# A hybrid encoder block on eight cores: the attention stage issued from one list of finer pieces, the key weights' load waiting for the first tile, and a new order of the prefix

## The chip, the cores and the metric

The kernel runs on all 8 cores of one Trainium2 chip, as one launch. Each core has a matrix engine (TensorE, PE in the profile), a vector engine (DVE), a scalar engine (ACT), a general engine (GpSimd, POOL) and a queue engine (SP) that issues transfers; transfers that convert float32 to bfloat16 on the way are issued by POOL. The engines run their own programs in order and wait for each other by semaphores. The time is that of the slowest core, in microseconds of the device; the kernel before had a median of 2082.74 us over 3 runs (2081.79, 2082.74 and 2295.69).

## The reference, cut to what matters

The input x has 4 sequences of 2048 tokens and 2048 channels. The part of the block that the change touches is the first half of the token mixer:

```
h = rms_norm(x, g_pre_mix)
a_x, a_b, a_c, q, k, v, og, a_lr, gate_a, gate_b = split(h @ w_in)
y_a = (a_b * causal_conv3(a_c * a_x)) @ w_a_out
log_a = log_sigmoid(a_lr @ w_alpha_up + b_alpha_up) / 16     # forget gate
b = cumsum(log_a) in chunks of 64 tokens
att = where(lower, (q e^(b-mid)) (k e^(mid-b))^T, (q e^(mid-b)) (k e^(b-mid))^T)
state = e^(b_last) * state + (k e^(b_last-b))^T v             # from chunk to chunk
o = rms_norm(att v + (q e^b) state) * head_gain * silu(og)
y_b = o @ w_b_out
x = x + rms_norm((sigmoid(gate_a) y_a + sigmoid(gate_b) y_b) @ w_mix_out)
```

There are 4 heads with keys of 128 and values of 256 channels. A SwiGLU mixer (5632 wide) and a gated embedding layer follow; the change doesn't touch them.

## The kernel before, in words

**Work of a core.** Two cores share a sequence. Each computes 1024 tokens, its own half. The second half needs the attention state that the first half leaves, so every core also reads the 1024 tokens before its own (`xp`, zeros on the first core of a pair), and forms only their decayed keys and from them the state: this is the **prefix**. The order of everything is that of the Python program: `P.emit` appends an instruction to its engine's program and works out the semaphores from the buffers that it reads and writes (`_needs`, L70). So the program text fixes both the order within each engine and which wait stands in front of which instruction.

**Prefix (L404 to L660).** Sixteen tiles of 128 tokens are loaded by SP, the 8 of `xp` first (numbers 0 to 7, tokens 512 to 1023 before tokens 0 to 511), then the 8 of `x`. A load is issued when the tile four before it was normalised (`t_norm`, L480). A string `ORDER` (L653) is walked word by word: S is a tile's square sum on ACT, X its scaling on DVE, T its 16 transposes on PE (two banks), V the two evictions on DVE, L and A the gate projection, z, c and e the gate, its scan and its factor for one head, a and b the keys of one head for the first and the second two tiles of a half (16 matmuls of 256 columns each), k and f the decayed keys and their transposes, G one of 16 products of prefix tokens with decayed keys (8 matmuls of 512 columns, evicted by ACT), D the four parts of the first decay (`Decay.one` to `four`), W the load of the query weights, C four small constants. The key weights come in four loads on POOL's queue (L501 to L504), followed on the same queue by the first value weights.

**Attention (L670 to L917).** `seed` forms the states of two heads. Then 4 steps (2 head pairs x 2 halves of the tokens) are run. A step has 12 **dense blocks** of 16 matmuls x 512 columns: q and k for two heads, 4 of v, 4 of the output gate og. The og blocks of a step run in the next step. Beside them it has 8 **units** (one head x 128 tokens): `near` (L797) is two score matmuls and two state updates on PE, then on DVE the mask, two copies and two updates of the state; `far` (L828) is three matmuls, then a square sum and rstd on ACT; `gated` is one DVE instruction that frees the bank of `far`; `out_flip` transposes for two heads. Each decay (`Decay`, L545) has one float32 matmul, ACT and DVE work and feeds the next q and k blocks; one set of factor tiles serves all. Dense blocks take turns on banks 0, 1, 2 (`dense`), all else on banks 3 to 7 in turn (`little`): a bank is handed out again five requests later and must be free by then.

Before, the loop at L875 ties these small pieces to numbered slots: a slot is one dense block, pieces registered by `ahead` are emitted in front of it, those by `after` behind it. `near` of a unit is in slot g, `far` in slot g+2, `gated` at the head of slot g+3.

**Convolution (L919 to L967).** For 8 channel groups and 2 halves three dense blocks each (x, C, B). The last step's og blocks and small pieces run into it. Weights come through a ring of 36,864 bytes per partition (`wload`), a load waiting for the readers of what it overwrites.

## Time and profile before

| | |
|---|---|
| median of 3 runs | 2082.74 us |
| the profiled execution's time | 2082.87 us |
| its span on the slowest core (core 6) | 2081.3 us |
| spans of the eight cores | 2064.5 to 2081.3 us |
| PE busy in the span | 1991.4 us (96%) |
| DVE, ACT, POOL busy | 582.5, 477.6, 155.4 us |
| mean granted clock of TensorE, by core | 0.989 to 0.993 |

The span is from the first to the last instruction of a core. PE idle is what is left beside its busy time, some 90 us of 2081. In this execution the prefix takes the first 133 us, attention runs up to about 388 us, and the convolution, whose first blocks stand among its last pieces, to about 520 us.

### The profile page before, as it was taken

To read this page: it belongs to the slowest core of one execution; us is meant where nothing else is said; L and a number is where in the kernel's file an instruction comes from. 1 tells how busy PE (TensorE), PEld (TensorE's weight loads), DVE (VectorE), ACT (ScalarE), POOL (GpSimd) and SP (SyncE) were. 2 spreads that over 40 slices of the span, in tenths; PEclk is the share of its full clock that TensorE was granted. 3 is DMA by queue.
4 is the path that set the end of the run, shared out by engine and by line. 5 is a ranking of instruction groups with operands and counts; after the bars stand their busy time and mean duration, and the time that the engine had idled before them with its cause. 6 is when DMAs were issued, how large, how long until landed. Compare 5 with 4: busy or idle time off the path is not lost.

```text
span 2081.3 us, 25824 instructions; the slowest of 8 cores (2064.5 to 2081.3 us)
## 1 busy us (share of the span) xinstructions
PE 1991.4 (96%) x10064; PEld 942.1 (45%) x10064; DVE 582.5 (28%) x911; ACT 477.6 (23%) x990; POOL 155.4 (7%) x185
## 2 busy tenths in 40 slices
PE   4999999999999999999799999999999999998896
PEld 3644455444444444444344444444444444444342
DVE  4836665433211111216310111110110011006416
ACT  4744553100111111116300000100000011014655
POOL 0011111000000000000000000000000000000233
PEclk9999999999999999999999999999999999999998
DMA  9830314554454543858564444434443454375353
GB/s 245 197 57 1 58 24 62 92 79 74 70 82 72 81 73 49 162 81 219 142 110 74 74 85 90 92 69 80 81 78 62 81 89 73 72 149 125 73 92 162
DMA packets 49796, 194.21 MB, mean 93 GB/s; under 512 B 3307, under 2 KB 4715, under 8 KB 43660
## 3 DMA queue, kind: packets, MB, share of 16 engines
q0 software_dynamic: 38688, 137.44, 40.0%
q1 hardware_dynamic: 10988, 55.13, 8.2%
q8 instruction: 81, 1.33, 0.2%
q14 instruction: 39, 0.32, 0.1%
HBM read 313.20 MB, written 16.78 MB: 159 GB/s over the span
## 4 chain that ended last, share of the span: by engine, by line
PE 89%; DMA 5%; DVE 3%; issue 2%; ACT 1%; DVEq 0%; POOL 0%; SPq 0%; ACTq 0%; POOLq 0%
PE bank L368 88%; ACT arena L356 1%; DMA arena<-w_ffu 1%; DMA arena<-w_k 1%; PE bank L376 1%; DVE arena L362 1%; DVE arena L359 1%; DMA arena<-w_ple 1%; DMA arena<-w_mix 1%; DMA arena<-xp 0%; DVE arena L407 0%; DVE arena L526 0%; DVE arena L818 0%; DVEq L158 0%; DVE arena L1065 0%
## 5 line engine op out<-in xcount | busy, mean ns | idle before, releaser
L368 PE MATMUL bank<-arena 128*128 128x512 bf16 (+3 forms) x9408 | 1957.9, 369 | 50.4 <-DVE arena L359 11.2
L368 PEld LDWEIGHTS bank<-arena 128*128 128x128 bf16 (+1 forms) x9408 | 899.9, 98 | 1084.2 <-issue 84.5
L359 DVE TENSOR_TENSOR arena<-bank,arena 128x512 f32<-128x512 f32 (+4 forms) x432 | 312.7, 738 | 1380.2 <-PE bank L368 1150.7
L356 ACT ACTIVATE arena<-bank 128x512 f32<-128x512 f32 (+8 forms) x408 | 227.0, 563 | 1482.6 <-PE bank L368 1089.0
L356 ACT ACTIVATE arena<-arena 128x1 f32<-128x1 f32 (+4 forms) x393 | 215.3, 563 | 68.3 <-DMA arena<-xp 18.0
L362 DVE SCALAR_TENSOR_TENSOR arena<-arena 128x512 f32<-128x512 f32 (+3 forms) x73 | 88.8, 1221 | 7.2 <-ACT arena L356 2.2
L344 POOL DMA_DIRECT2D arena<-w_ffu x44 | 31.4, 713 | 610.4 <-PE bank L368 428.9
L376 PE MATMUL bank<-arena 128*128 128x128 bf16 x656 | 51.0, 228 | 21.5 <-DVE arena L407 16.9
L376 PEld LDWEIGHTS bank<-arena 128*128 128x128 bf16 x656 | 44.4, 102 | 36.4 <-issue 26.3
L1364 POOL TENSOR_TENSOR arena<-arena 128x512 f32<-128x512 f32 x31 | 46.1, 1489 | 92.9 <-DVE arena L359 46.1
L362 DVE SCALAR_TENSOR_TENSOR arena<-bank,arena 128x256 bf16<-128x256 f32 (+1 forms) x64 | 33.2, 518 | 51.2 <-ACT arena L356 26.0
L359 DVE TENSOR_TENSOR arena<-arena 128x128 bf16<-128x128 bf16 (+2 forms) x81 | 40.9, 513 | 5.1 <-ACT arena L356 0.9
L344 POOL DMA_DIRECT2D arena<-w_gate x16 | 12.4, 772 | 322.7 <-PE bank L368 322.7
L794 POOL TENSOR_TENSOR arena<-arena 128x256 f32<-128x256 f32 x32 | 23.2, 726 | 140.4 <-DVE arena L359 138.1
L344 POOL DMA_DIRECT2D arena<-w_fd x16 | 11.9, 742 | 290.4 <-PE bank L368 271.0
L362 DVE SCALAR_TENSOR_TENSOR arena<-arena,bank 128x256 f32<-128x256 f32 x64 | 30.7, 480 | 9.3 <-DVE arena L818 4.7
L407 DVE TENSOR_SCALAR arena<-arena 128x2048 bf16<-128x2048 f32 x16 | 20.5, 1281 | 18.3 <-ACT arena L356 18.2
L818 DVE CAST arena<-arena 128x256 bf16<-128x256 f32 x64 | 24.2, 378 | 0.2 <-DVE arena L359 0.2
L356 ACT ACT_TABLE_LOAD x13 | 16.7, 1283 | 32.4 <-PE bank L368 30.3
L526 DVE TENSOR_TENSOR_SCAN arena<-arena 128x512 f32<-128x512 f32 x16 | 19.5, 1217 | 1.4 <-ACT arena L356 1.4
L356 ACT ACTIVATION_READ_ACCUMULATOR arena<-bank 128x1 f32 x96 | 18.8, 196 | 0.0
L344 POOL DMA_DIRECT2D arena<-w_conv x8 | 6.2, 780 | 125.9 <-PE bank L368 105.2
(30 smaller groups left out, 80.0 us busy)
## 6 DMA issues: line engine op xcount, KB each, us to landing
arena<-w_ffu POOLq DMA_DIRECT2D x44, 1024.0 KB, 8.5
arena<-w_gate POOLq DMA_DIRECT2D x16, 1536.0 KB, 13.7
arena<-w_fd POOLq DMA_DIRECT2D x16, 1408.0 KB, 11.1
arena<-x SPq DMA_DIRECT2D x16, 1024.0 KB, 9.7
arena<-w_conv POOLq DMA_DIRECT2D x8, 1536.0 KB, 13.7
arena<-xp SPq DMA_DIRECT2D x8, 1024.0 KB, 12.8
arena<-w_mix POOLq DMA_DIRECT2D x4, 2048.0 KB, 17.2
x1s<-arena SPq DMA_DIRECT2D x8, 1024.0 KB, 12.5
```

The costliest lines, as they stand in the source:

```text
L344: P.dma("pool", f"w{j}", lambda e: e.dma_start(out=flat, in_=src, max_dma_last_dim=8192), writes=[buf, wsems[j]])
L356: P.emit("act", lambda e: e.activation(out=out, in_=in_, func=func, **kw), reads=reads, writes=writes, partw=partw)
L359: P.emit("dve", lambda e: e.tensor_tensor(out=out, in0=in0, in1=in1, op=op), reads=reads, writes=writes, partw=partw)
L362: P.emit("dve", lambda e: e.scalar_tensor_tensor(out=out, in0=in0, scalar=scalar, in1=in1, op0=op0, op1=op1), reads=reads, writes=writes, ...
L368: P.emit("pe", lambda e, l=l, r=r, j=j: e.matmul(out_ap, lhsT=l, rhs=r, start=(start and j == 0), stop=(stop and j == n - 1)), reads=reads ...
L376: P.emit("pe", lambda e, j=j, a=a: e.transpose(out=ptv[:, j * 128:(j + 1) * 128], in_=a, identity=ident), reads=list(reads) + [tb0] if j = ...
L407: P.emit("dve", lambda e: e.tensor_scalar(out=xn, in0=x, scalar1=stats[:, i, 2:3], scalar2=None, op0=ALU.mult), reads=[xbuf, stb[i]], writ ...
L526: P.emit("dve", lambda e: e.tensor_tensor_scan(out=out, data0=data0, data1=data1, initial=0.0, op0=ALU.mult, op1=ALU.add), reads=reads, wr ...
L794: P.emit("pool", lambda e, o=o: e.tensor_tensor(out=o, in0=o, in1=hgb, op=ALU.mult), reads=[cb], writes=[SOb[i]])
L818: P.emit("dve", lambda e, n=n: e.tensor_copy(out=sbf_r[n].ap, in_=S[:, h, :]), reads=[Sb[h]], writes=[sbfb[n]])
L1364: P.emit("pool", lambda e: e.tensor_tensor(out=out, in0=sg, in1=gbs_r[s].ap, op=ALU.mult), reads=[sb_, gbs_b[s]], writes=wr, partw=part)
```

## The change

The key weights' four loads wait for tile 0 in place of tile 1. The prefix's list is a new one; its pieces are the same, in another order. The slots of the attention stage go: their place is taken by a second list, `ORDER2`, walked as the first is. `near` is split: its PE part is N, its DVE part M (`state`); the tail of an og block is l (`og_rest`). F, g, t, K are `far`, `gated`, `out_flip`, `k_flip`; d is a part of a decay, four to each; s a seed; w a weight load (w0 value weights and w1 gate weights of the second head pair, w2 the first convolution weights); Z takes the convolution's memory; X, C, B are its first blocks. The number of a q, k word counts 2 to a step, of v, o, l, t 4, of N, M, F, g 8. The last 36 blocks of the convolution keep their order. The amount of work is the same. Cut to its core:

```diff
-        P.dma("pool", f"wf_wk{h}", lambda e, h=h: e.dma_start(out=wk_r.ap[:, h * 2048:(h + 1) * 2048], in_=w_k[h], max_dma_last_dim=8192), after=[xin[1][1]], writes=[wkb[h]])
+        P.dma("pool", f"wf_wk{h}", lambda e, h=h: e.dma_start(out=wk_r.ap[:, h * 2048:(h + 1) * 2048], in_=w_k[h], max_dma_last_dim=8192), after=[xin[0][1]], writes=[wkb[h]])
...
-    ORDER = """S0 X0 S1 S2 X1 T0 S3 V0 T1 X2 V1 T2 S4 X3 a0 a1 V2 X4 S5 T3 a2 V3 T4 V4 S6 L0 b1 X5 T5 V5 S7 X6 H z0
-        X7 c0 z1 a3 c1 T6 e0 z2 z3 V6 b2 T7 V7 c3 c2 S8 b0 S9 X8 b3 k0 e2 e1 L1 T8 V8 S10 z4 f0 a4 X9 T9 S11 C
-        e3 z5 k1 b4 k2 f2 V9 f1 a5 X10 T10 c4 e4 k3 a6 b6 X11 k4 z6 b5 c5 V10 c6 f3 e5 z7 T11 f4 k5 S12 V11 a7
-        b7 f5 c7 v e6 X12 e7 A0 k6 k7 f6 T12 f7 W S13 E V12 D0 G0 G1 S14 G2 X13 X14 G3 G4 G5 G6 T14 V14 T13 D1
-        G7 S15 V13 G8 D2 G9 G10 X15 G11 G12 T15 G13 V15 G14 A1 G15 D3"""
+    ORDER = """S0 X0 S1 X1 S2 S3 T0 V0 T1 S4 X2 T2 S5 V1 X3 a0 T3 V2 a1 V3 X4 L0 S6 X5 T4 a2 V4 z0 X6 c0 z1 S7 b0 b2 T6 T5 S8
+        c1 e0 V6 e1 X7 z3 b1 V5 T7 V7 k0 k1 z2 c2 S9 H a3 X8 L1 a4 T8 e2 c3 V8 S10 a5 X9 f0 z5 z4 k2 b4 b3 X10 e3 f1 T9
+        a6 c5 S11 f2 C V9 T10 c4 X11 z6 b5 k3 a7 V10 e5 c6 f3 e4 e6 z7 k4 b7 k5 T11 V11 S12 b6 c7 f4 f5 k6 e7 X12 A0 v W
+        k7 f6 f7 T12 S13 E G0 X13 G1 S14 G2 G3 G4 X14 V12 G5 D0 G6 D1 T13 S15 G7 G8 T14 X15 V13 V14 D2 D3 G9 G10 G11 G12
+        T15 G13 V15 G14 G15 A1"""
...
-            def late():
-                tt(sg, bk[:, :], sg, ALU.mult, [bb, SOb[i]], [SOb[i]])
-                for hh in range(2):
-                    o = sg[:, hh * 256:(hh + 1) * 256]
-                    P.emit("pool", lambda e, o=o: e.tensor_tensor(out=o, in0=o, in1=hgb, op=ALU.mult), reads=[cb], writes=[SOb[i]])
-
-            ahead(slot["n"] + 1, late)
+            self.gb[i] = (bk, bb)
+
+        def og_rest(self, i):
+            bk, bb = self.gb[i]
+            sg = SO_r[i].ap
+            tt(sg, bk[:, :], sg, ALU.mult, [bb, SOb[i]], [SOb[i]])
+            for hh in range(2):
+                o = sg[:, hh * 256:(hh + 1) * 256]
+                P.emit("pool", lambda e, o=o: e.tensor_tensor(out=o, in0=o, in1=hgb, op=ALU.mult), reads=[cb], writes=[SOb[i]])
...
+            self.nb[(hh, i)] = us
+
+        def state(self, hh, i):
+
+            h = self.pair * 2 + hh
+            a_, t_ = i % 2, self.unit(hh, i) % 3
+            us = self.nb[(hh, i)]
+            bk, bb, _ = us[0]
...
-    for n, stp in enumerate(steps):
-        stp.wv, stp.wo = wv_of[stp.pair], wo_of.get(stp.pair)
-        mid = [lambda i=i, p=steps[n - 1]: p.og_block(i) for i in range(4)] if n > 0 else [lambda: stp.v_block(0), lambda: stp.v_block(1)]
-        blocks = [lambda: stp.q_block(0), lambda: stp.k_block(0)] + mid + [lambda: stp.q_block(1), lambda: stp.k_block(1)]
-        blocks += [lambda i=i: stp.v_block(i) for i in range(0 if n > 0 else 2, 4)]
-        g0 = slot["n"]
-        q1 = g0 + 2 + len(mid)
-        nxt = g0 + len(blocks)
-        d1 = decays[2 * n + 1]
-        for g, f in ((g0 + 1, lambda d=d1: d.one(little)), (g0 + 2, d1.two), (g0 + 3, d1.three), (q1 - 1, d1.four), (g0 + 3, lambda p=stp: p.k_flip(0)), (q1 + 3, lambda p=stp: p.k_flip(1))):
-            after(g, f)
-        if n < 3:
-            d0 = decays[2 * n + 2]
-            for g, f in ((q1 + 1, lambda d=d0: d.one(little)), (q1 + 2, d0.two), (q1 + 3, d0.three), (nxt - 1, d0.four)):
-                after(g, f)
-        for u, (hh, i) in enumerate([(hh, i) for hh in range(2) for i in range(4)]):
-            g = nxt + 2 + u
-            ahead(g + 3, lambda p=stp, a=hh, i=i: p.gated(a, i))
-            if hh == 1:
-                after(g + 4, lambda p=stp, i=i: p.out_flip(i))
-            after(g + 2, lambda p=stp, a=hh, i=i: p.far(a, i))
-            after(g, lambda p=stp, a=hh, i=i: p.near(a, i))
-        for blk in blocks:
-            pre()
-            blk()
-            run_small()
-        if n == 2:
-            seed(1)
-        if n == 1:
+    conv_w = []
+
+    def load(n):
+        if n == 0:
             load_v(1)
-        if n == 2:
+        elif n == 1:
             load_o(1)
-            steps[2].wo = steps[3].wo = wo_of[1]
...
+    def load(n):
+        if n == 0:
             load_v(1)
-        if n == 2:
+        elif n == 1:
             load_o(1)
-            steps[2].wo = steps[3].wo = wo_of[1]
-    conv_w = [wload(w_conv[0])]
-    for i in range(4):
-        pre()
-        steps[3].og_block(i)
-        run_small()
-
-
-    M.drop(wk_r, wal_r, wq_r, GT_r[1], aug_r)
-    ua_r = M.take_at(B0 + 5632, 16384, BF16, "p (k t) -> p k t", k=8)
-    ua = ua_r.ap
-    uab = ua_r.buf("ua")
-    ux_r = [M.take(2048, F32) for _ in range(2)]
-    uxb = [r.buf(f"ux{j}") for j, r in enumerate(ux_r)]
-    u_r = [M.take(514 * 4, F32) for _ in range(2)]
-    ub_ = [r.buf(f"u{j}") for j, r in enumerate(u_r)]
-    y_r = [M.take(2048, F32) for _ in range(2)]
-    yb = [r.buf(f"y{j}") for j, r in enumerate(y_r)]
-    hal_r = M.take(64, F32)
-    halb = hal_r.buf("hal")
-
-    for cc in range(8):
-        if cc > 0:
-            conv_w.append(wload(w_conv[cc]))
+        else:
+            conv_w.append(wload(w_conv[n - 2]))
...
+    def conv_room(n):
+        M.drop(wk_r, wal_r, wq_r, GT_r[1], aug_r)
+        r = M.take_at(B0 + 5632, 16384, BF16, "p (k t) -> p k t", k=8)
+        cv["ua"], cv["uab"] = r, r.buf("ua")
+        for name, size in (("ux", 2048), ("u", 514 * 4), ("y", 2048)):
+            rs = [M.take(size, F32) for _ in range(2)]
+            cv[name], cv[name + "b"] = rs, [r.buf(f"{name}{j}") for j, r in enumerate(rs)]
+        cv["hal"] = M.take(64, F32)
+        cv["halb"] = cv["hal"].buf("hal")
...
+    def conv_x(cc, half):
+        if cc >= len(conv_w):
+            load(cc + 2)
+        wx, _, _, wb, ts, hb = conv_of(cc, half)
+        bk, bb = dense.next()
+        mm(bk[:, :], bb, [(wx[:, k, :], hT[:, k, ts]) for k in range(16)], [wb, hb])
+        act(cv["ux"][half].ap, bk[:, :], AF.Copy, [bb], [cv["uxb"][half]])
...
+    DO2 = {"q": step_of(Step.q_block, 2), "k": step_of(Step.k_block, 2), "v": step_of(Step.v_block, 4), "o": step_of(Step.og_block, 4),
+           "l": step_of(Step.og_rest, 4), "K": step_of(Step.k_flip, 2), "t": step_of(Step.out_flip, 4),
+           "N": step_of(lambda p, u: p.near(u // 4, u % 4), 8), "M": step_of(lambda p, u: p.state(u // 4, u % 4), 8),
+           "F": step_of(lambda p, u: p.far(u // 4, u % 4), 8), "g": step_of(lambda p, u: p.gated(u // 4, u % 4), 8),
+           "d": lambda n: (lambda: decays[n // 4].one(little), decays[n // 4].two, decays[n // 4].three, decays[n // 4].four)[n % 4](),
+           "s": lambda n: seed(n), "w": load, "Z": conv_room, "X": lambda n: conv_x(n // 2, n % 2), "C": lambda n: conv_c(n // 2, n % 2), "B": lambda n: conv_b(n // 2, n % 2)}
+    ORDER2 = """q0 k0 v0 d4 d5 d6 q1 k1 d7 K0 v2 d8 v1 d9 K1 d10 N0 q2 v6 N1 M0 M1 o0 l0 F0 d11 k2 N2 v3 d12 g0 M2 K2 o1 N3 N4
+        o2 d13 M3 F1 M4 l2 F2 o3 N5 l1 M5 d14 F3 g1 g2 l3 q3 d15 k3 d16 v5 N6 F4 v4 M6 g3 d17 F5 g4 d18 N7 K3 g5 M7 v7
+        N8 M8 q4 F6 g6 d19 F7 k4 g7 t1 d20 w0 t0 t2 d21 o4 F8 l4 d22 q5 t3 o5 g8 N9 M9 l5 o6 N10 M10 o7 N11 M11 N12 F9
+        l6 v9 l7 g9 F10 M12 k5 K4 F11 g10 d23 N13 M13 g11 v10 d24 d25 d26 q6 w1 N14 M14 F12 v8 g12 d27 k6 N15 o8 F13 l8
+        t4 g13 v11 F14 s1 M15 g14 d28 N16 M16 K5 v12 N17 M17 N18 F15 M18 o9 F16 o10 t5 t6 l9 d29 g15 g16 F17 v14 l10 N19
+        M19 t7 F18 d30 g17 o11 g18 N20 F19 M20 q7 K6 F20 N21 l11 v15 g19 g20 o12 N22 M21 M22 t8 l12 v13 d31 N23 F21 g21
+        M23 k7 F22 g22 Z o13 N24 F23 o14 M24 N25 g23 M25 F24 K7 w2 o15 N26 l13 M26 X0 t10 g24 N27 l14 l15 C0 M27 t9 F25
+        B0 N28 M28 g25 F26 g26 X1 C1 N29 M29 F27 t11 F28 g27 B1 F29 g28 N30 g29 X2 M30 N31 M31 C2 F30 t12 B2 g30 F31 X3
+        t14 g31 C3 t15 B3 t13"""
+    for word in ORDER2.split():
+        DO2[word[0]](int(word[1:] or 0))
+    for n in range(4, 16):
+        conv_x(n // 2, n % 2)
+        conv_c(n // 2, n % 2)
+        conv_b(n // 2, n % 2)
```

## Rows read from the trace of the kernel before

**Rows 1.** Page, part 4: shares of the chain that ended last.

```profile
PE 89%; DMA 5%; DVE 3%; issue 2%; ACT 1%; DVEq 0%; POOL 0%; SPq 0%; ACTq 0%; POOLq 0%
```

**Rows 2.** Windows: stretch, length, each engine's busy us, TensorE clock, DMA share, GB/s.

```profile
0.00:40.00 40.00, 13.78 (x92) 10.81 (x93) 15.13 (x16) 18.34 (x30) 4.54 (x10) 1.00 0.93 252
40.00:133.00 93.00, 90.31 (x665) 55.15 (x662) 61.77 (x66) 55.11 (x94) 2.56 (x3) 1.00 0.76 165
133.00:400.00 267.00, 257.68 (x1477) 130.90 (x1478) 156.21 (x349) 111.05 (x278) 35.33 (x51) 1.00 0.28 44
```

**Rows 3.** Waits of PE, whole span: releaser, total us, times, longest.

```profile
PE bank L376 <- DVE arena L407: 16.9, 4, 13.3
...
PE bank L368 <- DMA arena<-w_k: 10.4, 3, 6.4
...
PE bank L368 <- DVE arena L362: 9.1, 11, 1.3
...
PE bank L368 <- ACT arena L356: 1.0, 1, 1.0
```

**Rows 4.** Timeline of PE, prefix: start, us, work, idle before and its releaser.

```profile
13.28 1.86 PE L376 MATMUL bank<-arena 128*128 128x128 bf16 x16 [13.28 <-DVE arena L407]
...
25.46 3.57 PE L368 MATMUL bank<-arena 128*128 128x256 bf16 x16 [3.19 <-DMA arena<-w_k]
35.39 3.57 PE L368 MATMUL bank<-arena 128*128 128x256 bf16 x16 [6.36 <-DMA arena<-w_k]
38.76 1.87 PE L376 MATMUL bank<-arena 128*128 128x128 bf16 x16
41.51 1.91 PE L368 MATMUL bank<-arena 128*128 128x256 bf16 x16 [0.89 <-DMA arena<-w_k]
43.26 1.06 PE L376 MATMUL bank<-arena 128*128 128x128 bf16 x16
44.24 5.47 PE L368 MATMUL bank<-arena 128*16 128x512 bf16 x32
```

**Rows 5.** Timeline of POOL: the key weights' loads.

```profile
13.35 0.73 POOL L504 DMA_DIRECT2D arena<-w_k  x1 [12.65 <-DMA arena<-xp]
...
16.91 0.77 POOL L344 DMA_DIRECT2D arena<-w_v  x1
```

**Rows 6.** Tile w_k: its transfers.

```profile
DMA to landing us min/median/max: 11.9/23.4/31.8
```

**Rows 7.** Timeline of ACT: square sums of two tiles.

```profile
9.04 1.91 ACT L356 ACTIVATE arena<-arena 128x2048 bf16<-128x2048 f32 x1 [6.25 <-DMA arena<-xp]
...
12.82 1.91 ACT L356 ACTIVATE arena<-arena 128x2048 bf16<-128x2048 f32 x1 [1.19 <-DMA arena<-xp]
```

**Rows 8.** Timeline of DVE, prefix.

```profile
39.92 2.35 DVE L359 TENSOR_TENSOR arena<-bank,arena 128x1024 bf16<-128x1024 bf16 x2 [10.03 <-PE bank L376]
```

**Rows 9.** Timeline of PE: end of prefix, and attention.

```profile
133.20 18.63 PE L368 MATMUL bank<-arena 128*128 128x256 bf16 x98 [1.03 <-ACT arena L356]
...
191.95 8.38 PE L368 MATMUL bank<-arena 128*128 128x256 bf16 x46 [0.73 <-DVE arena L362]
201.33 9.54 PE L368 MATMUL bank<-arena 128*128 128x256 bf16 x48 [1.00 <-DVE arena L362]
212.20 0.27 PE L368 MATMUL bank<-arena 128*128 128x256 bf16 x1 [1.33 <-DVE arena L362]
...
212.53 3.62 PE L368 MATMUL bank<-arena 128*128 128x512 bf16 x16
```

**Rows 10.** Timeline of DVE in the same stretch.

```profile
191.32 0.48 DVE L362 SCALAR_TENSOR_TENSOR arena<-bank,arena 128x256 bf16<-128x256 f32 x1 [0.85 <-ACT arena L356]
...
196.06 2.54 DVE L362 SCALAR_TENSOR_TENSOR arena<-bank,arena 128x512 bf16<-128x512 f32 x4
...
200.70 0.48 DVE L362 SCALAR_TENSOR_TENSOR arena<-bank,arena 128x256 bf16<-128x256 f32 x1
```

**Rows 11.** Tile w_conv: its transfers.

```profile
DMA to landing us min/median/max: 13.3/13.7/23.3
```

More of the change, by code:

```diff
@@ L732, in __init__ @@
             self.sb = {}
[L733 removed]
+            self.ob, self.nb, self.gb = {}, {}, {}
             self.ts = slice(self.half * 512, (self.half + 1) * 512)
@@ L804, in near @@
             ts = slice(i * 128, (i + 1) * 128)
-            a_, t_ = i % 2, self.unit(hh, i) % 3
             bk, bb = little.next()
@@ new lines, in step_of, with go @@
+    def step_of(f, per):
+        def go(n):
+            stp = steps[n // per]
+            stp.wv, stp.wo = wv_of.get(stp.pair), wo_of.get(stp.pair)
+            f(stp, n % per)
+        return go
+    cv = {}
+    def conv_room(n):
[7 more added lines that the diff above has]
+        cv["halb"] = cv["hal"].buf("hal")
```

77 lines of the change are left out of this document (29 added, 48 removed).

## The prediction

> **What bounds the kernel now.** I read the chain of waits first: 89% of the chain that ended last is PE's own work [rows 1], so only time in which PE stands idle, or runs at half pace, can be had, since the change leaves the amount of its work alone. Then the windows, to see where the idle time is [rows 2]: of the first 40 us PE is busy for 13.8, so 26.2 are idle; of the next 93 us 2.7 are idle; of the 267 us of attention 9.3. From 400 us on nothing is touched but the place in time. The whole stake is thus 26.2 + 2.7 + 9.3 = 38.2 us, or 1.8% of 2083. Last I read PE's waits and its timeline for what ends each gap. Over the span, 16.9 us are waits for a scaled tile, 13.3 of them for the very first, which no order can bring before its load; 10.4 us are waits for the key weights; 9.1 us, in 11 waits, are for DVE instructions of line 362; 1.0 us is one wait for ACT [rows 3]. The last two are the attention stage and its entrance.
>
> **Key weights, and the order up to them.** POOL issues the first key load at 13.35 us, when tile 1 is in; the first value weights follow on the same queue at 16.91 [rows 5]. ACT starts on tile 0 at 9.04 and on tile 1 at 12.82 [rows 7], so the new wait ends 3.8 us sooner and POOL, which has nothing else to do then, issues all five loads (and that of the narrow gate weights) 3.8 us sooner. The quickest key load took 11.9 us and the slowest 31.8 [rows 6]: the transfers share a system that is 93% busy over the first 40 us [rows 2]. PE met the first three at 25.46, 35.39 and 41.51 after waiting 3.19, 6.36 and 0.89 us [rows 4]. What a key load gains is between nothing (the new tiles that the other changes let in take its share) and the 3.8 us by which it starts sooner. The new list also lets tiles in sooner: it scales tile 5 ahead of the eviction of tile 4 on DVE, where before DVE stood still for 10.03 us behind tile 3's transposes, which stood behind the second keys on PE [rows 8, 4], and with it stood SP's next load. So the shares get narrower just when keys three and four are on their way, and I take 1.3 us, nearer to the lower end.
>
> More certain is what PE does before it needs the third keys. Before, T4 and L0 came after a2; in the new list T3 goes ahead of a1, and L0 and T4 ahead of a2. L0 is 16 matmuls of 512 columns: the row of 32 matmuls at 44.24 us holds it and one key group, so 5.47 - 1.91 = 3.6 us; T4 is 16 transposes, 1.0 us at full pace [rows 4]. This is 4.6 us of work brought into time that was idle. From a2 on PE had only 2.7 us of gaps up to 133 us [rows 2], so what it is ahead there it stays ahead, if DVE keeps up: **prefix 4.6 + 1.3 = 5.9 us**, bounds 0 and 10.4 + 2.7 = 13. The upper is all waits for key weights and all later gaps. The lower is nothing, and not a loss: DVE is busy for 61.8 of the 93 us after 40 [rows 2], its work is the same, and 31 us of slack can absorb a worse order of scans and evictions locally.
>
> The trace shows 524 KB landing in the first key load's 11.9 us while the core moved 252 GB/s [rows 6, 2], 3.0 MB: some 17% went to it. The Trainium skill ("DMA: Bandwidth & Descriptors", Queues, rings and completion order) says that each DMA engine takes turns between the queues that have work, packet by packet. The trace agrees that the queues share, but not that they do so half and half by bytes; halves would put the first keys in 4.2 us after their issue, and all waits for them would go, which is the upper bound above.
>
> **Clock.** The first two key groups took 3.57 us each for 16 matmuls of 256 columns, the third 1.91; 16 transposes 1.87 against 1.06 [rows 4]. That is the pace of 1.2 and of 2.4 GHz. Bringing the early work closer together may turn the pace sooner, at most 1.7 us per key group before the third; since a2 waits for its weights anyway, I cost it at nothing.
>
> **Entrance to attention.** The seeds wait 1.03 us for ACT's eviction of the last product [rows 9, 3]. The new list ends G14 G15 A1; A1 is 16 matmuls like L0, 3.6 us, and covers it: **1.0 us**. The last part of the first decay, D3, stands earlier too; q0 needs it two seeds' time later in either case. The new list has one block (v0) instead of two between k0 and q1, so q1's eviction waits for the second decay's factors, but the bank of q1 is asked for again only by v1, three blocks after, 10.9 us at 3.62 us a block [rows 9]: nothing.
>
> **Attention.** The 11 waits for line 362 come in a pattern of about 0.7, 1.0 and 1.3 us in three of the four steps, where the next step's first blocks run [rows 9]. What ends them is `gated`: DVE's instructions at 191.32 and 200.70 take 0.48 us each and PE starts 0.15 us behind their ends, at 191.95 and 201.33 [rows 9, 10]. The bank of a `far` is asked for five requests later, in the second slot after; `gated` is emitted in time, but stands on DVE behind the state updates and a q eviction of 2.54 us, or a k one [rows 10]. I went through the new list by hand, counting requests of banks 3 to 7 from each F to the fifth after it: g stands ahead of that request each time, mostly with a dense block between, and big evictions are placed after M and g of the unit in hand, not before. DVE has the capacity, 156 of 267 us [rows 2]. The new waits are small ones on ACT: F then g at once (F6 g6) holds DVE about 1 us, which nobody waits for at that moment. I keep 2 us of idle time for places that I missed: **9.1 - 2.1 = 7.0 us**; bounds +9.1 and, below nothing, see the fourth rival.
>
> **Transfers in the attention stage.** POOL's program has in order the output gates' products (two per l) and the weight loads. w0 waits for v7, the first reader of it is v9, seven dense blocks later (25 us); w1 waits for o7, its reader o8 comes six blocks later (22 us). w2, the first convolution weights, waits for v13 and stands behind l12; X0 reads it after k7, o13, o14, o15, four blocks (14.5 us), and small pieces of 6,656 columns (four N, four F, one K), 2.9 us at a block's pace of 8,192 columns in 3.62: 17.4 us. The convolution's loads took 13.3 to 23.3 us, 13.7 in the median [rows 11]: with 0.8 us of issue, as for the value weights [rows 5], that is hidden at the median, and 6.7 us late at the slow end. I take 0 (the median decides), and keep 7 for the range. The second and third convolution loads keep at least five blocks. The `l` on DVE waits for ACT's three passes behind an og block, as the old emission at the next slot's head did: nothing.
>
> **Sum.** Prefix 5.9, entrance 1.0, attention 7.0: 13.9 us less. The profiled execution took 2082.87 us, 1.6 beside its span, and the median is 2082.74, so they are the same for this purpose: 2082.7 - 13.9 = 2068.8. The stages after it wait as before, with some us of chance in their weight transfers.
>
> **The rivals.**
> 1. *More than that*: key loads come by half shares, as the page's rule has it, and no bank is late: 13 + 1 + 9 = 23 less, 2060. For it: the third keys came 6.1 us behind the second, against 9.9 us for the second behind the first [rows 4], so shares do change. Against: the 17% above. Chance 0.12.
> 2. *The prefix gives only its entrance*: the keys are hidden behind tiles in any order, and DVE, busy for 66% of the 93 us after 40 and surely more in their first part, where the scans, the key products and most evictions are, sets the pace as soon as PE gets ahead: 1 + 7 = 8 less, 2075. Chance 0.17.
> 3. *The waits in attention only move*, from `gated` to M or to q evictions: 5.9 + 1.0 = 6.9 less, 2076; with rival 2 as well, 2082. Together 0.19.
> 4. *Slower*: the five small banks. N takes two at once and only M frees them; in the slots N and M came once per block, in the list come runs as N3 N4 or N17 M17 N18. If DVE is late with M by as much as it was with `gated` before, 0.83 us (9.1 / 11), in each of the 32 units, idle time is 26.6 us in place of 9.1, 17.5 more; with no prefix gain 2100, with it 2093. It decides from 20 late units on (16.6 us, more than the 9.1 now idle and the 6.9 gained elsewhere). Against it: DVE has 111 us to spare in the stage, and nearly every unit has a dense block beside it. Chance 0.06.
> 5. *Nothing is changed in effect*, since the issue at tile 0 meets a full system and the list reproduces the slots: within 2 us of 2083. The list visibly differs; counted in the 2082 of rival 3.
>
> The forecast itself has 0.46: 2064 to 2073.
>
> **How the numbers follow.** 2068.8 is the likeliest. Cutting off the last of rival 1 below and rival 4 with some of rival 3 above gives 2060 to 2081, with the late convolution load inside. A change of 2% is 42 us, about what a measurement of this kernel can tell from none; the whole stake was 38. So faster by over 2% has 0.01, slower by over 2% (2124) 0.02: it would need rival 4 twice over. Within 2%: 0.97.
>
> **What would show it.** After the change: the first key load issued near 9.6 us; PE at the third keys (a2) at 36 to 41 us with L0 and T4 behind it; the seeds starting near 126 in place of 133.2, without the wait for ACT; waits for line 362 down from 9.1 to about 2 us; no wait for w_conv, and no new wait of PE for DVE line 359 in the stage. I am wrong if PE's idle time between 40 and 133 us grows by more than 3 us (DVE sets the pace), if attention keeps 6 us or more of waits, or if later stages shift by more than 5 us.

## The result, and the profile after

The changed kernel takes 0.991 of the time before, 95% interval [0.9887, 0.9932]: 2061.8, 2062.6 and 2064.2 us against 2080.6 to 2082.7. (The median of its first five runs is 2267.2, because in three of them the granted clock of one die was 0.81 to 0.90 in the mean, which happens to the kernel before as well; the comparison leaves such runs out.) The forecast was 2068.8, range 2060 to 2081. The slowest core's span is 2061.0 us, where it was 2081.3: **20.3 us less, forecast 13.9**. (The ratio of the times makes it 18.7.)

The page: busy time by engine, then the shares of the chain that ended last.

```profile
PE 1987.0 (96%) x10064; PEld 941.0 (46%) x10064; DVE 579.3 (28%) x911; ACT 478.6 (23%) x990; POOL 156.9 (8%) x185
PE 90%; DMA 6%; DVE 1%; issue 1%; ACT 1%; DVEq 0%; POOL 0%; SPq 0%; ACTq 0%; POOLq 0%
```

PE bounds it still [rows 1]. Windows, with the columns of [rows 2] (length, then busy us of PE, PE's loads, DVE, ACT and POOL; clock; DMA share; GB/s):

```profile
0.00:40.00 40.00, 17.80 (x117) 11.92 (x118) 18.61 (x18) 16.04 (x27) 4.52 (x10) 0.91 0.94 245
40.00:133.00 93.00, 92.10 (x687) 57.71 (x685) 58.51 (x63) 58.59 (x100) 8.12 (x13) 1.00 0.78 174
133.00:400.00 267.00, 267.00 (x1514) 134.36 (x1513) 159.87 (x360) 111.48 (x277) 31.53 (x42) 1.00 0.31 46
28.00:36.00 8.00, 4.50 (x29) 2.73 (x26) 5.13 (x5) 4.07 (x7) 0.00 (x0) 0.62 1.00 248
```

PE is busy for 4.0 us more of the first 40, 1.8 more of the next 93, and for all 267 of attention, where it was idle for 9.3. In the last row it is granted 1.2 GHz for most of 8 us; the record has the fall at 29.95 us, 1.3 us into the wait that is left. PE's waits over the span:

```profile
PE bank L376 <- DVE arena L407: 18.3, 4, 13.5
PE bank L368 <- DVE arena L359: 11.9, 7, 5.1
PE bank L368 <- DMA arena<-w_k: 3.5, 1, 3.5
PE bank L368 <- ACT arena L356: 0.2, 1, 0.2
```

Lines for L362 (9.1 us before [rows 3]) are gone; key weights went from 10.4 to 3.5 and ACT from 1.0 to 0.2, while the waits for scaled tiles (L407) grew from 16.9 to 18.3. The prefix on PE and POOL (start, us, work, idle before and its releaser), which answers to [rows 4, 5]:

```profile
21.45 1.86 PE L376 MATMUL bank<-arena 128*128 128x128 bf16 x16 [2.85 <-DVE arena L407]
23.71 3.27 PE L368 MATMUL bank<-arena 128*128 128x256 bf16 x16 [0.40 <-DVE arena L359]
27.56 1.05 PE L376 MATMUL bank<-arena 128*128 128x128 bf16 x16 [0.58 <-DVE arena L407]
32.12 7.68 PE L368 MATMUL bank<-arena 128*128 128x256 bf16 x32 [3.50 <-DMA arena<-w_k]
39.73 1.07 PE L376 MATMUL bank<-arena 128*128 128x128 bf16 x16
40.63 7.42 PE L368 MATMUL bank<-arena 128*128 128x256 bf16 x52
...
9.76 0.73 POOL L504 DMA_DIRECT2D arena<-w_k  x1 [9.06 <-DMA arena<-xp]
13.32 0.76 POOL L344 DMA_DIRECT2D arena<-w_v  x1
```

The first key load leaves at 9.76 instead of 13.35; the second keys (with L0 in the same row) start at 32.12 instead of 35.39; the third at 40.63 instead of 41.51, with L0 and T4 now done.

**Where the 20.3 us are.** Two instructions of POOL mark the stages: its clearing behind the first seeds ("seeds' end"), and its first w_gate load, which ends the attention stretch. First the kernel before (core 6), then after (core 0):

```profile
137.04 1.45 POOL L721 MEMSET arena<- 128x512 bf16 x3 [0.67 <-PE bank L368]
481.24 0.77 POOL L344 DMA_DIRECT2D arena<-w_gate  x1 [20.75 <-PE bank L368]
```
```profile
130.46 1.92 POOL L721 MEMSET arena<- 128x512 bf16 x4 [3.13 <-PE bank L368]
463.79 0.78 POOL L344 DMA_DIRECT2D arena<-w_gate  x1 [20.75 <-PE bank L368]
```

Up to seeds' end 6.6 us less; the stretch 344.2 before and 333.3 after, 10.9 less; the rest of the kernel, 1600.1 and 1597.2, 2.9 less. The rest is untouched code whose weight transfers vary by some us: in the median core it takes 1592.6 before and 1589.9 after, and 1587.3 to 1590.8 in the twelve kernels below that share it. So the trace of before is the longest of all there, and some 2 of the 20.3 us may be chance. The marks are steadier than a total, so the experiments are read by them. Medians over the eight cores, us; "keys" is PE's start on each of the first three key groups:

| kernel | first w_k issue | keys 1, 2, 3 | seeds' end | stretch |
|---|---|---|---|---|
| before | 13.2 | 25.7, 35.4, 41.7 | 137.3 | 344.2 |
| after | 9.5 | 23.7, 32.0, 40.0 | 130.6 | 333.3 |
| attention alone | 13.5 | 26.0, 35.8, 42.7 | 139.8 | 333.3 |
| + early issue | 9.5 | 23.2, 32.5, 38.7 | 134.3 | 333.3 |
| + prefix list | 13.4 | 25.9, 35.7, 44.3 | 134.1 | 333.3 |
| slots, gated early | 13.1 | | 139.1 | 344.1 |
| slots, spread | | | 137.7 | 336.6 |
| M joined to N | | | 130.2 | 347.7 |
| gated late | | | 130.2 | 347.2 |
| A1 first | | 3: 40.7 | 131.9 | 333.3 |
| keys without wait | 1.6 | 30.8, 35.5, 43.4 | 141.2 | 333.3 |
| fillers | 9.6 | 23.2, 32.3, 38.6 | 130.3 | 333.3 |
| values late | | 3: 40.1 | 130.2 | 333.3 |
| both of these | | 3: 38.4 | 129.1 | 333.3 |

### The profile page after: what moved, and what is told of

Read it like the earlier page. It is cut to its first block, busy times and chain, and to the rows that moved or that the text cites. A ratio compares the mean times of both kernels' runs of the same rounds, so it can differ in the third digit from the quotient of the medians.

```text
span 2061.0 us, 25873 instructions; the slowest of 8 cores (2046.4 to 2061.0 us)
## 1 busy us (share of the span) xinstructions
PE 1987.0 (96%) x10064; PEld 941.0 (46%) x10064; DVE 579.3 (28%) x911; ACT 478.6 (23%) x990; POOL 156.9 (8%) x185
## 4 chain that ended last, share of the span: by engine, by line
PE 90%; DMA 6%; DVE 1%; issue 1%; ACT 1%; DVEq 0%; POOL 0%; SPq 0%; ACTq 0%; POOLq 0%
PE bank L368 89%; DMA arena<-w_mix 2%; DMA arena<-w_ffu 2%; PE bank L376 1%; DMA arena<-w_k 1%; DMA arena<-w_ple 1%; ACT arena L356 1%; DVE arena L359 1%; DVE arena L362 1%; DMA arena<-xp 0%; DVE arena L1056 0%; DVEq L148 0%; DVE arena L407 0%; SPq L388 0%; POOL arena L504 0%
## 5 line engine op out<-in xcount | busy, mean ns | idle before, releaser
L368 PE MATMUL bank<-arena 128*128 128x512 bf16 (+3 forms) x9408 | 1953.6, 369 | 34.9 <-DVE arena L359 11.9
L362 DVE SCALAR_TENSOR_TENSOR arena<-arena 128x512 f32<-128x512 f32 (+3 forms) x73 | 88.8, 1221 | 7.1 <-ACT arena L356 2.2
L376 PE MATMUL bank<-arena 128*128 128x128 bf16 x656 | 49.8, 226 | 21.0 <-DVE arena L407 18.3
L376 PEld LDWEIGHTS bank<-arena 128*128 128x128 bf16 x656 | 43.4, 101 | 34.6 <-issue 25.6
L362 DVE SCALAR_TENSOR_TENSOR arena<-bank,arena 128x256 bf16<-128x256 f32 (+1 forms) x64 | 32.4, 517 | 31.9 <-PE bank L368 21.2
L344 POOL DMA_DIRECT2D arena<-w_fd x16 | 11.9, 744 | 290.3 <-PE bank L368 271.0
L362 DVE SCALAR_TENSOR_TENSOR arena<-arena,bank 128x256 f32<-128x256 f32 x64 | 30.7, 480 | 8.9 <-DVE arena L827 4.8
L407 DVE TENSOR_SCALAR arena<-arena 128x2048 bf16<-128x2048 f32 x16 | 20.5, 1283 | 28.4 <-ACT arena L356 28.4
L827 DVE CAST arena<-arena 128x256 bf16<-128x256 f32 x64 | 19.6, 307 | 1.6 <-PE bank L368 1.6
L356 ACT ACTIVATION_READ_ACCUMULATOR arena<-bank 128x1 f32 x96 | 18.7, 195 | 0.0
## 6 DMA issues: line engine op xcount, KB each, us to landing
arena<-w_gate POOLq DMA_DIRECT2D x16, 1536.0 KB, 13.2
arena<-w_conv POOLq DMA_DIRECT2D x8, 1536.0 KB, 13.2
x1s<-arena SPq DMA_DIRECT2D x8, 1024.0 KB, 11.9
```

The source lines that it names most:

```text
L344: P.dma("pool", f"w{j}", lambda e: e.dma_start(out=flat, in_=src, max_dma_last_dim=8192), writes=[buf, wsems[j]])
L356: P.emit("act", lambda e: e.activation(out=out, in_=in_, func=func, **kw), reads=reads, writes=writes, partw=partw)
L362: P.emit("dve", lambda e: e.scalar_tensor_tensor(out=out, in0=in0, scalar=scalar, in1=in1, op0=op0, op1=op1), reads=reads, writes=writes, ...
L368: P.emit("pe", lambda e, l=l, r=r, j=j: e.matmul(out_ap, lhsT=l, rhs=r, start=(start and j == 0), stop=(stop and j == n - 1)), reads=reads ...
L376: P.emit("pe", lambda e, j=j, a=a: e.transpose(out=ptv[:, j * 128:(j + 1) * 128], in_=a, identity=ident), reads=list(reads) + [tb0] if j = ...
L407: P.emit("dve", lambda e: e.tensor_scalar(out=xn, in0=x, scalar1=stats[:, i, 2:3], scalar2=None, op0=ALU.mult), reads=[xbuf, stb[i]], writ ...
```

## The experiments

**The three parts, one at a time.** *attn_only* is the changed kernel with the old list of the prefix and the old wait of the key loads. The next two each give one of them back.

```
attn_only:     ORDER = """S0 X0 S1 S2 X1 T0 ..."""  (the old one)   and   after=[xin[1][1]]
p_issue_only:  ORDER = """S0 X0 S1 S2 X1 T0 ..."""  (the old one)
p_list_only:   after=[xin[1][1]]
```

> The old prefix (old list, key weights' loads behind tile 1) with the new attention list. Theory: the attention stage alone gives what it gave in the changed kernel. There the stretch from the end of the first seeds (POOL's clearing at 137.04 us before, 130.46 after) to the first load of the gate weights (481.24 and 463.79) fell from 344.2 to 333.3 us, by 10.9. So here that stretch should be 333 to 334 us, PE's waits for line 362 none, the prefix as before (seeds' end near 137 us), and the whole 10 to 11 us under the kernel before, near 2072 by the profiled span, a ratio of 0.995. Rival: the two parts lean on each other, since the attention list fits the state in which the new prefix leaves DVE and ACT; then the stretch is 336 us or more and waits come back at its start.

Measured 0.9943 [0.9923, 0.9962]. The stretch is 333.3 as expected, and no wait of PE for line 362 is left in it: attention's 10.9 us need nothing of the prefix.

> The changed kernel with the old list in the prefix, the key weights' loads still behind tile 0. It shows against the run with both old what the earlier issue alone gives. Theory: the old list meets all its first key groups as soon as their weights land (waits of 3.2, 6.4 and 0.9 us before), so an issue 3.6 us sooner moves PE by what the landings move: the second keys 2 to 3.6 us sooner, the third 1 to 3; the seeds' end at 134 to 136 in place of 137.0. Rival A: the full transfer system gives the keys' landings nothing, seeds' end 137. Rival B: the earlier issue is the whole of the prefix's gain, seeds' end near 130.5.

Measured 0.9941 [0.9918, 0.9963], seeds' end 134.3, as expected.

> The changed kernel with the key weights' loads behind tile 1 again, the new list kept. Theory: the list alone keeps L0 and T4 ahead of the third keys and the last eviction hidden (4.6 + 1.2 us), but the wait before the second keys grows from 3.5 us by up to 3.6. As a2 waited for nothing in the changed kernel, the later landing shows nearly whole: seeds' end 131.5 to 134 in place of 130.5. Rival A: the issue doesn't matter, seeds' end 130.5 as in the changed kernel. Rival B: the list alone gives nothing, seeds' end near 137.

Measured 0.9915 [0.9888, 0.9942], seeds' end 134.1, just outside what was expected. In the profile one core took 343.1 us for the stretch, at a lower clock and with PE busy throughout (core 3, windows):

```profile
140.00:340.00 200.00, 200.00 (x1038) 98.42 (x1037) 122.53 (x276) 93.89 (x224) 22.82 (x30) 0.95 0.16 30
```

Against the changed kernel's 130.6, the early issue is worth 3.5 us and the list 3.7 with the other in place; both together are worth 6.7 (137.3 to 130.6). The old prefix itself ended between 137.3 and 139.8 in four kernels that share it, the new one between 130.2 and 130.6 in three. So what each part gives alone is less exact: 3.0 to 5.5 for the issue, 3.2 to 5.7 for the list; and both together could be up to 9.6.

**Is it `gated` that was late?** The kernel before, with `gated` emitted right behind its `far`, a slot's head earlier.

```diff
-            ahead(g + 3, lambda p=stp, a=hh, i=i: p.gated(a, i))
...
             after(g + 2, lambda p=stp, a=hh, i=i: p.far(a, i))
+            after(g + 2, lambda p=stp, a=hh, i=i: p.gated(a, i))
```

> The kernel before with one thing moved: the instruction that frees the bank of far (gated) is emitted right behind far in slot g+2, no longer at the head of slot g+3. All else is the old slots and the old prefix. Theory: the 11 stops of PE in attention are banks held until gated has passed the q and k evictions on DVE; with gated ahead of them at least 8 of the 11 stops go, the stretch from seeds' end to the first gate weights' load falls from 344.2 to 333 to 336 us, and the old slots would have done as well as the new list. DVE then waits about 1 us for ACT in each unit, which has room (156 of 267 us busy). Rival: the stops are a lack of DVE time where a step's end meets the next one's start; then they only change their name, waits for other DVE instructions (359, 818) take the place of those for 362, and the stretch stays at 341 to 346.

Measured 0.9979 [0.996, 0.9997]; the stretch is 344.1 on five cores, 342.4 on three. The forecast of 333 to 336 fell. PE (core 0), its windows there, and DVE (core 2):

```profile
192.20 8.38 PE L368 MATMUL bank<-arena 128*128 128x256 bf16 x46 [0.74 <-DVE arena L362]
201.18 0.27 PE L368 MATMUL bank<-arena 128*128 128x256 bf16 x1 [0.59 <-DVE arena L362]
202.30 3.92 PE L368 MATMUL bank<-arena 33*128 33x512 f32 x10 [0.86 <-DVE arena L359]
```
```profile
190.00:203.00 13.00, 10.81 (x60) 5.44 (x57) 10.27 (x28) 5.49 (x20) 2.91 (x4) 1.00 0.01 2
203.00:209.00 6.00, 6.00 (x23) 2.50 (x23) 4.47 (x11) 1.49 (x3) 0.00 (x0) 0.72 0.00 0
```
```profile
194.21 0.48 DVE L362 SCALAR_TENSOR_TENSOR arena<-bank,arena 128x256 bf16<-128x256 f32 x1 [3.52 <-ACT arena L356]
```

Nine waits stay. Put earlier, `gated` stands at DVE's head while ACT hasn't its factors yet: DVE waits 3.52 us for ACT with the state updates queued behind it, and now a bank that line 359 frees is late too. After the three stops the clock fell (0.72 in the mean over the next 6 us), and again near 258 us. This hides a gain. By the spacing of PE's starts the nine stops cost 7.6 us, where the eleven cost 10.9; each fall of the clock, 3.4 us at half, gave back some 1.5. The three cores with 342.4 have the same stops and only the second fall. So moving `gated` up took 3.3 us of stops away, and the clock took back 1.4 to 3.1 of them.

**The slots, but looser.** The kernel before, with the second head's four units two slots later, nothing else.

```diff
-            g = nxt + 2 + u
+            g = nxt + 2 + u + (2 if u >= 4 else 0)
```

> The kernel before with one line of its slots changed: of the 8 units of a step the last four run two slots later, so that no unit stands in the two slots in which the next step's second q and k blocks are evicted. Theory, as it stands after the run with gated moved: the stops come where DVE is wanted for all of the time (10.0 of 10 us busy in the stretch that holds them, three times, and 2.8 to 3.8 of 10 us in the v blocks between); what the new list does is to level this. Then this levels it too: DVE's fullest 10 us fall below 9.5, the stretch from seeds' end to the first gate weights' load falls from 344.2 to 333 to 337 us, with at most 3 stops. Rival (order within a unit is what counts: N and M apart, gated ahead of evictions): the stops move with the units and the stretch stays above 340.

Measured 0.9957 [0.9939, 0.9975]; stretch 336.6: 7.6 of the 10.9 us come with this one line. Three stops are left, in three of the four steps, and no core's clock falls in the stage (core 6, PE):

```profile
192.65 16.56 PE L368 MATMUL bank<-arena 128*128 128x256 bf16 x81 [0.74 <-DVE arena L362]
244.16 16.56 PE L368 MATMUL bank<-arena 128*128 128x256 bf16 x81 [0.99 <-DVE arena L362]
299.16 1.13 PE L368 MATMUL bank<-arena 128*128 128x256 bf16 x5 [0.99 <-DVE arena L362]
```

One thing in that expectation has to be put right: its "busy for all of the 10 us" summed instructions that overlap by some 0.07 us each. The windows view counts DVE's busy time in the stretch from 187 to 197 us as 8.49 of 10 us before and 8.42 here; counted like this the fullest 10 us of the stage are 9.33 before, 8.96 after, 9.33 here, 8.96 in *joined* and 8.59 in *late_gated*. How full DVE is doesn't tell kernels with stops from kernels without, so the levelling that was expected didn't happen, though the gain did. What I take the spreading to give is lead: time between the emission of the instruction that frees a bank and the next request of that bank. This run alone doesn't show that; the next two test it, each for one kind of bank.

**M joined to N.** The changed kernel with each state update right behind its `near`, where the data allow it. (By the two lists, 20 of the 32 stood apart and 3 do now; the expectation counted 16 and 3.)

```diff
-    ... o2 d13 M3 F1 M4 l2 F2 o3 N5 l1 M5 d14 F3 g1 g2 l3 q3 ...
+    ... o2 d13 F1 M4 l2 F2 o3 N5 M5 l1 d14 F3 g1 g2 l3 q3 ...
```

> The changed kernel with M put right behind its N wherever the order of the data allows it (16 of the 32 were apart, by up to two dense blocks; 13 of them are joined). Theory (levelled demand for DVE is what counts): DVE does the same work at nearly the same places, the stretch stays at 333.3 to 334.5 us. Rival (splitting near into N and M is what removed the stops): stops of 0.5 to 1.5 us come back at most of the 13, and the stretch is 338 us or more.

One profiled run: stretch 347.7, worse than before the change. PE, DVE, PE's waits in the stage and windows (core 6):

```profile
192.00 10.34 PE L368 MATMUL bank<-arena 128*128 128x512 bf16 x36 [2.68 <-DVE arena L359]
```
```profile
188.99 0.42 DVE L359 TENSOR_TENSOR arena<-bank,arena 128x256 bf16<-128x256 f32 x1 [0.66 <-PE bank L368]
...
191.17 0.68 DVE L359 TENSOR_TENSOR arena<-bank,arena 128x512 f32<-128x512 f32 x1
```
```profile
PE bank L368 <- DVE arena L359: 9.2, 4, 3.0
```
```profile
188.00:198.00 10.00, 7.32 (x32) 3.12 (x30) 4.98 (x12) 5.22 (x14) 4.48 (x6) 0.83 0.00 1
```

The dense bank of o1 is freed by l1, the product at 191.17. M5 used to stand behind it; now M5 starts at 188.99 and l1 runs behind its six instructions, and PE, at q3, has waited 2.68 us for that bank. DVE is busy for half of those 10 us: it is the order on it, not its load. The stop costs twice, since the clock falls behind it (0.83), on six of the eight cores. My theory, that joining levels DVE's demand and costs nothing, fell. The rival held in its price (338 or more), not in its form: there are five stops, four of them of 1.3 to 3.0 us, and not small ones at most of the units joined.

**Gated late.** The changed kernel with each `gated` one dense block later, where requests of its bank allow.

```diff
-    ... N5 l1 M5 d14 F3 g1 g2 l3 q3 d15 ... v5 N6 F4 v4 M6 g3 d17 F5 g4 d18 N7 K3 g5 M7 v7
+    ... N5 l1 M5 d14 F3 l3 q3 g2 g1 d15 ... v5 N6 F4 v4 M6 g3 d17 F5 d18 N7 K3 M7 v7 g5 g4
```

> The changed kernel with 28 of the 32 gated one dense block later, each still ahead of the fifth request for its bank in the program's order. Theory (bank held by far until gated, in a levelled DVE): a part of the far banks is asked for before gated has run, so stops come back, each ended by line 362, 0.2 to 1.5 us; but not where DVE has room: a stretch of 335 to 339 us. If the levelling is all, it stays at 333.3 to 334. If banks are all, 28 stops of 0.8 us make it 355.

One profiled run: stretch 347.2, against 335 to 339 expected. It is few long stops, not many short ones: six of them cost 10.1 us by the spacing of starts, and two falls of the clock about 3.4 more. The longest, PE and then DVE (core 1):

```profile
309.87 9.74 PE L368 MATMUL bank<-arena 128*128 128x256 bf16 x43 [2.98 <-DVE arena L362]
```
```profile
306.78 2.94 DVE L362 SCALAR_TENSOR_TENSOR arena<-bank,arena 128x512 bf16<-128x512 f32 x5 [1.63 <-PE bank L368]
```

The row of DVE is a q eviction and the `gated` that now stands behind it. So lead of `gated` matters in this list, which *slots_gated_early* alone couldn't show.

**A1 first.** The last words `G14 G15 A1` turned to `G14 A1 G15`.

> The changed kernel with the last two pieces of the prefix exchanged, A1 then G15, as before. Theory: A1 behind G15 hides ACT's eviction of the last product from the seeds; exchanged, PE waits 1.0 us and stands 1.2 us longer (1.03 and 0.16 of a matmul's tail, as before), seeds' end near 131.8 in place of 130.6 in the median of the cores. Rival: the eviction is hidden anyway, seeds' end 130.6.

One profiled run: seeds' end 131.9, 1.3 later, as expected. The wait for ACT is back (start of the seeds, PE):

```profile
128.57 7.75 PE L368 MATMUL bank<-arena 128*128 128x256 bf16 x51 [1.14 <-ACT arena L356]
```

**Keys without any wait.** The changed kernel, `after=[xin[0][1]]` taken out, so that the loads leave at 1.6 us.

> The changed kernel with no wait at all before the key weights' loads: they are issued at about 1 us, with the first tiles. Theory (transfers share a full system; what counts is the first moment at which tiles and keys are both there): the first tiles come later, T0 at 15 to 18 us in place of 13.5, the keys' waits (3.5 us in the changed kernel) go, seeds' end 129.5 to 132.5, about the same as the changed kernel's 130.6. Rival (the earlier the keys the better, as the step from tile 1 to tile 0 gave 3.5 us): seeds' end near 127.

Measured 2071.4 and 2075.9 us against 2079.1 to 2087.0 before, too few for an interval. Seeds' end 141.2, worse than either theory gave. PE and ACT (core 1):

```profile
17.68 1.86 PE L376 MATMUL bank<-arena 128*128 128x128 bf16 x16 [17.68 <-DVE arena L407]
```
```profile
13.44 1.91 ACT L356 ACTIVATE arena<-arena 128x2048 bf16<-128x2048 f32 x1 [10.64 <-DMA arena<-xp]
```

The key loads landed 11.6, 22.7 and 30.8 us (least, median, most) after their issue; they had taken 11.9, 23.4 and 31.8 before [rows 6] and take 12.7, 24.2 and 32.5 after. A key load keeps its time whenever it is issued, and the tiles pay: tile 0 is on ACT at 13.44 instead of 9.04 [rows 7]. Wait for tile 1, tile 0, nothing: seeds' end 134.1, 130.6, 141.2.

Why it keeps its time can be read from the packets of the two queues. In the kernel before, from 34 to 45 us (core 6; queue 0 is POOL's, queue 1 is SP's; packets, MB, share of the engines):

```profile
q0 software_dynamic: 255, 0.94, 51.5%
q1 hardware_dynamic: 255, 1.87, 48.5%
```

The queues move packet for packet. A data packet of a key load writes 4 KB (bf16), one of a tile 8 KB, so the keys get a third of the bytes. The first key load waits 4.1 to 4.9 us from its issue to its first packet and 7.0 to 8.8 from there to its landing (1.4 to 1.8 and 8.7 to 9.8 when it is issued at 1.6 us). It is also seen why the second keys are so late. The narrow gate weights are issued between the first two key loads, and their 64 KB go in 128 packets of 512 bytes, as many as a key load has: 9.2 to 10.3 us pass between the landings of the first and second key loads, before and after, and 5.7 to 7.7 between the second and third. By estimate from these, issuing the gate weights behind the second key load would bring the second keys some 4 us sooner. That wasn't tried.

**Fillers.** Matmuls without use (line 651, 80, 14, 14 and 40 of them) put where PE waits in the first 30 us, to raise the clock.

```diff
-    ORDER = """S0 X0 S1 X1 S2 S3 T0 V0 T1 S4 X2 T2 S5 V1 X3 a0 T3 V2 a1 ...
+    ORDER = """S0 X0 S1 X1 S2 S3 Y80 T0 Y14 V0 T1 Y14 S4 X2 T2 S5 V1 X3 a0 T3 Y40 V2 a1 ...
```

> The changed kernel with matmuls of no use put where PE waits in the prefix: 80 of 128 columns ahead of T0, 14 behind T0 and T1, 40 behind T3, all on constants and into a bank that nobody reads; the results are the same. In the changed kernel the records show TensorE granted half its clock for 3.4 to 6.8 us from about 31 us on, right behind its wait of 3.5 us for the second keys, and T0 to T2 at half pace. Theory: with PE kept at work the granted clock stays whole there, a1 and L0 run at 1.74 and 3.45 us, and since PE waits for nothing behind them the 1.7 to 3.4 us come off the end of the prefix: seeds' end 127.5 to 129.5 in place of 130.6. Rival: the half clock has another cause (power of the whole core, a fixed time after the start); then it falls at the same time, and seeds' end is 130.6 or, where fillers stand in the way of a1, later.

Measured 0.9901 [0.9875, 0.9927]. PE (core 6):

```profile
32.20 5.46 PE L368 MATMUL bank<-arena 128*128 128x256 bf16 x32 [0.91 <-DMA arena<-w_k]
...
49.22 2.95 PE L368 MATMUL bank<-arena 33*128 33x512 f32 x18 [1.23 <-DVE arena L359]
```

a1 with L0 takes 5.46 us, the full pace, on seven of the eight cores, instead of 7.68 (7.1 in the median core), and the third keys start 1.4 sooner (38.6). The fillers don't keep the clock up throughout: each core's record has a fall between 14 and 28 us, ahead of a1. Seeds' end, expected at 127.5 to 129.5, moves by 0.3 only: from 49 us on PE waits for what comes of the next tiles. ACT waits for tile 8 then (first the changed kernel, then this one):

```profile
52.55 1.91 ACT L356 ACTIVATE arena<-arena 128x2048 bf16<-128x2048 f32 x1 [3.85 <-DMA arena<-x]
```
```profile
53.21 1.91 ACT L356 ACTIVATE arena<-arena 128x2048 bf16<-128x2048 f32 x1 [3.88 <-DMA arena<-x]
```

**Values late**, to give the tiles those shares: the first value weights wait for tile 12; and both together.

```diff
-        flat, wb = wload(w_v[pair])
+        flat, wb = wload(w_v[pair], [xin[12][1]] if pair == 0 else ())
```

> The changed kernel with the first value weights' load, which stands behind the key weights on POOL's queue and is needed only by the seeds near 127 us, made to wait until tile 12 is in. Theory: with the fillers PE stood 1.35 us earlier at the third keys and lost it again, DVE waiting for ACT and ACT for tiles (3.9 us for tile 8), while the transfers were at full share up to 80 us; so from 40 to 80 us the tiles set the pace, and the value weights take a share from them. Held back, tiles 8 to 10 come sooner, and the small stops of PE between 40 and 100 us go: seeds' end 0.5 to 2 us sooner than 130.6. Rival (nothing is lost there, PE has no stop over 1 us behind the second keys): seeds' end 130.6 within 0.3. Against both: value and query weights would be too late for the seeds; then seeds' end is later than 131.

Measured 0.9902 [0.9887, 0.9917], seeds' end 130.2, 0.4 sooner, where 0.5 to 2 was expected.

> The same with the fillers of the run before. Theory: the whole clock at the second keys gives 1.35 us at a2, and now the tiles are there to keep it: seeds' end 127 to 129, and the fastest kernel so far by 1 to 3 us (2059 to 2061, ratio 0.989). Rival: DVE's own work is the bound between 40 and 90 us (51 of 60 us busy); then seeds' end stays at 130 as with the fillers alone.

Measured 0.99 [0.9885, 0.9915], seeds' end 129.1, 1.5 sooner. Tile 8 is on ACT 3.5 us sooner than in the changed kernel:

```profile
49.09 1.91 ACT L356 ACTIVATE arena<-arena 128x2048 bf16<-128x2048 f32 x1 [0.35 <-DMA arena<-x]
```

So in the first 50 us pace and tiles seem to bound together. Each alone gives 0.3 or 0.4, which can't be told from nothing: *joined* and *late_gated*, with the changed kernel's own prefix, also end at 130.2. Both give 1.5, or 1.1 against those two. In total (2059.5 to 2061.0) the gain over the changed kernel isn't clear either.

## Why the prediction was right, and where it wasn't

**The whole.** PE's idle time was the stake, and it was won where the prediction looked for it. The times lie in the stated range, but two of the three are below the band of 2064 to 2073 that had the chance of 0.46, between it and the first rival. By the spans the sum was 6.4 us short. The attention term was 3.9 too small, and 2.9 came from stages that weren't in the sum. The prefix came out right by luck: two of its terms were wrong in opposite directions.

**Attention, forecast 7.0, measured 10.9.** Two causes. The 2.1 us kept for places missed weren't needed: no wait is left. And a stop costs more than its idle time. By the spacing of PE's starts the 11 stops of before are 10.91 us, where their idle time is 9.1: the last 128x256 matmul ahead of a stop stands in the record with about 0.27 us, while within a run the next starts 0.109 us after it, so about 0.16 us more is lost at each, 11 x 0.16 = 1.8 us. The forecast took the waits' column for the price.

**Its reason, `gated`, was only half of it.** `gated` was late on DVE, and in the new list it must not be later (*late_gated*). Put earlier in the slots, it takes away 3.3 of the 10.9 us of stops and loses most of that to the clock (*slots_gated_early*). What frees the banks of the blocks must have its lead too (*joined*). Most of the gain (7.6) is the looser spacing of the units, which the slots could have had.

**The prefix, forecast 5.9 + 1.0, measured 6.7 in the medians of these two traces: right in sum by two errors of opposite sign.** The step "4.6 us of work brought into time that was idle" was wrong as put. L0 and T4 come ahead of a2 but behind a1, while most of the idle time was ahead of a1. From keys 2 to keys 3 it was 6.3 us before (with T3 at half pace [rows 4] between) and is 8.0 after, so of the 4.6 us, 1.7 stay on the path and 2.9 are gained. The gain is about what left the path between the two: T3, which now goes ahead of a1 (1.9 us), and the wait for the third keys (0.9). With the old issue it is 8.6, so 2.3 gained. On the other side the early issue was undersized: forecast 1.3, but keys 2 start 3.4 us sooner, close to the whole 3.8 that was my upper bound. I had expected the new tiles to take the keys' share; the landing times and packet counts above say that a key load keeps its time. 3.4 + 2.9 = 6.3 at keys 3; with the entrance 7.3, of which 6.7 arrive. The same reckoning gives 3.0 for the issue alone (keys 3 at 38.7 for 41.7; measured 3.0) and 2.0 + 1.0 for the list alone (keys 3 at 44.3, 2.6 later, with 4.6 done; measured 3.2).

**Entrance, 1.0:** held. The wait went from 1.03 to 0.2, and with A1 put back ahead of G15 it is 1.14.

**Clock, costed at nothing:** wrong in detail. Around the wait of 3.5 us for w_k PE was granted half its clock (0.62 in the mean from 28 to 36 us) and a1 with L0 took 7.68 us where 5.46 is full pace, 2.2 us (1.6 in the median core). But the cost is hidden behind the tiles to 0.3 us or less, as *fillers* shows, so nothing was the right price for the total.

**The rivals.** The first (2060) gave nearly the time, and one half of it came: no bank is late. Its other half, key loads by half shares, didn't: one wait of 3.5 us for keys is left. The time came near by another way, with 2.9 us from the rest of the kernel that no step explains and that are within its chance. The second fell: PE is idle for 0.9 us from 40 to 133. The third and fourth fell: no wait of PE is left in the stage, for M or anything else. *joined* shows that the fourth's mechanism was near in kind, with other banks: dense ones, not the small ones. The Trainium skill ("DMA: Bandwidth & Descriptors", Queues, rings and completion order) has each DMA engine take turns between the queues packet by packet, and the trace agrees: 255 packets of each queue in 11 us. Halves of the bytes were my own reading of it, and wrong, since a key packet writes 4 KB and a tile packet 8 KB. My figure of 17% was counted from the issue, with 4.5 us in it before the load's first packet moved.

**What stays open.** Which placements in the new list are needed, beyond those tried; and where in the untouched stages the 2.9 us lie. An early `gated` whose wait for ACT is free wasn't tried, nor were the narrow gate weights behind the second keys.

## What to carry to other kernels

Where an engine in order frees another's banks, ask for each bank how far ahead of its next request the freeing instruction is emitted, and what stands before it on its engine; neither the engine's load nor its nearest late instruction answers that. When work is moved into idle time, check on which side of the wait it lands: only what goes ahead of the longest wait is free. A load that shares the system with the first tiles has a best start: sooner by one tile gained 3.5 us, sooner by one more lost 10.6.
